# A two-layer hybrid trunk on one Trainium2 core: state-space blocks gathered by group before their products, first normed tiles placed between the row products, rotary tables and masks placed behind the last normed tile, and further hand-overs rearranged

## The chip, the cores and the metric

The kernel runs on one core of one Trainium2 chip. TensorE (PE) multiplies matrices, VectorE (DVE), ScalarE (ACT) and GpSimd (POOL) work element by element, and SyncE (SP) issues most DMA transfers; each engine follows its own list of instructions in order and waits on semaphores that the others raise. The metric is the device time of one execution in microseconds. Lower is better.

## The reference

The input x has 1024 tokens of width 1024. Two layers follow one another and a final RMSNorm ends the trunk. One layer is:

```python
mod = silu(c) @ w_ada[l] + b_ada[l]                  # six vectors of 1024: sh1, sc1, g1, sh2, sc2, g2
h = rms_norm(x, norm1_g[l]) * (1.0 + sc1) + sh1
z = h @ w_in[l]                                      # 1024 -> 512 + 256 + 128 + 32 + 1024 + 1024
u, cq_in, ckv_in, kr_in, gate_a, gate_b = split(z)
# (A) S5 mixer: 32 groups of 16 channels, 64 complex states each, a scan over the tokens
h_t = Abar * h_(t-1) + Bbar @ u_t ;  y = Re(C @ h_t) + d * u_t
y_a = (gelu(y) * sigmoid(gelu(y) @ w_glu + b_glu)) @ w_a_out
# (B) latent attention: 8 heads, 64 + 32 rotary columns, causal by positions, masked softmax
y_b = mla_mixer(cq_in, ckv_in, kr_in, positions, cos, sin, ...) @ w_b_out
merged = sigmoid(gate_a) * y_a + sigmoid(gate_b) * y_b
x = x + g1 * (merged @ w_out[l])
h = rms_norm(x, norm2_g[l]) * (1.0 + sc2) + sh2
x = x + g2 * ((silu(h @ w_gate[l]) * (h @ w_up[l])) @ w_down[l])   # inner width 2816
```

## The kernel before, in words

**Layout and precision.** Activations lie transposed, channels on the partitions: x_sb, h_hi and h_lo hold 8 tiles of 128 channels by 1024 tokens. A token half is 512 columns, half 0 and half 1. Every large product is made of three fp32r products (`products`, L550, L552, L553): weights and data are each cut into a rounded part (hi) and the remainder (lo), and hi times hi, hi times lo and lo times hi are added in PSUM. PSUM has 8 banks of 512 fp32 columns; `pair(b)` is the two banks from b on.

**Weight units.** Weights come in units of 128 x 1024 with two slots (unit number modulo 2). SP loads the raw fp32 of a unit (`load_unit`, L538, two transfers) once the remainder of unit n - 2 is made; ScalarE rounds it (`split_hi`, L526) once the raw data is there and TensorE is through with unit n - 2; GpSimd makes the remainder (`split_lo`, L534); TensorE starts the unit after `unit_ready`, which waits for the remainder. ScalarE's order inside the loops thus decides when the next unit's weights are there.

**Start.** For layer 0 VectorE makes the first two modulation vectors from rows of w_ada (`row_products`, 16 of them, SP loads the rows into the four places of ada_rows), the rotary tables after row 5 (`rope_tables`), two of the eight mask blocks after row 10 (`mask_rows`; ScalarE adds to each in `mask_block`), and two weight remainders. Then it makes normed tiles: `norm_inverse`, `hidden_scaled` and `hidden_lo` (L2032, L2042) for tile k of half o, in the order H_ORDER, with ScalarE's rounding `hidden_hi` (L1564) in between. Six mask blocks follow (L1986), and then a chain of 95 dependent small steps on [128, 32] values (`s5`, from L2077), which gives the discretised state-space parameters; ScalarE adds Exp and one Sin (L1613) to it.

**u.** TensorE makes u for half 0 while the tiles come in (`u_products`), then half 1. ScalarE evicts u in 8 steps (U_ORDER, u_t). In layer 0 ScalarE comes to them behind its mask blocks, and in both layers behind the Sin and the split of the first gate unit.

**Gate units and state-space batches.** The 16 gate units (U_GATE + t, two halves each) fill the time in which the state-space part is made. It goes by eight batches of four groups, each in four steps of half a unit (`s5_part`, part 0 to 3 at step h, b = (h - S5_LAG) / 4, with a lag of 6 half units in layer 0 and 4 in layer 1). On TensorE part 0 is `batch_transposes` (L1156: blocks be, which GpSimd makes at L933), part 1 `batch_states` (L1168, after ScalarE has copied the blocks mt, L1536, `batch_transposed`), part 3 `batch_outputs` (L1186 and L1187). The Toeplitz blocks that L1186 needs go from toe_col through DMA to toe[partition, j, r, m, g] (`batch_toeplitz`), where g, the group, is the innermost axis: the weights of one group are read 4 elements apart. L1187 reads its weights as one stretch. VectorE makes the running states with `states(b)` (L2173 and others), after TensorE's part 1, and the turned powers of the next batch.

**SP beside the gate units.** For unit t, SP issues in this order: the unit's weights, a pair of adaLN tiles (`ada_pair(t - 3)`, L642; each of the two waits until VectorE has used an earlier tile of the three in ada_raw), and for odd t `ut_load` (L703, four transfers, u by groups). VectorE uses the adaLN tiles in products that stand behind `states(b)` in its order.

**Attention.** `side_of(step)` says which query, key or value product stands between which score steps; the first pair of heads takes its values and odd keys at its steps 0 to 2.

**Merge, projection, FFN.** A merge unit multiplies attention (o_hi, o_lo) and state-space outputs (yg_hi, yg_lo) by their projection. x is spilled to HBM during a layer's first half and comes back in one transfer (x_back) ahead of the output projection, where ScalarE makes squares for the second norm. The FFN goes by chunks of two 128-row tiles: gate and up products with two bank pairs each, then `down_products`, whose eight output tiles use two bank pairs in turn, each evicted into x_sb by VectorE (L2420). Six units of weights belong to each chunk.

## Time and profile before

| | us |
|---|---|
| median of three runs | 3154.01 |
| lowest, highest | 3153.0, 3155.38 |
| profiled execution | 3150.09 |
| its span, first to last instruction | 3147.9 |
| PE busy | 3044.4 (97%) |
| PE weight load busy | 2559.9 (81%) |
| DVE busy | 1546.8 (49%) |
| ACT busy | 986.5 (31%) |
| POOL busy | 870.6 (28%) |

The mean clock granted to TensorE is 0.987 of full speed. The span of the profiled execution is 2.2 us shorter than its time: the rest lies ahead of the first instruction and behind the last. "Busy" adds up the instructions of an engine with overlaps counted once. In a row of the profile "L1168" is line 1168 of the kernel, "ps<-ut,mt" means that ps is written from ut and mt, the shapes follow in the same order, and a bracket such as [7.51 <-PE ps L1168] says that the engine stood idle for 7.51 us before the instruction and that PE's line 1168 ended the wait ("issue" is a wait that the profile puts down to nothing). All times are us from the start of the span unless ns is written.

### The profile page before, as it was taken

What the parts mean: (1) busy time and instruction counts of PE and PEld (TensorE: products, weight loads), DVE (VectorE), ACT (ScalarE), POOL (GpSimd) and SP (SyncE); (2) the same over time, 40 slices, a digit from 0 to 9 for tenths busy, and PEclk for the clock granted to TensorE, in tenths of its full rate; (3) what the DMA queues carried; (4) which work ended last, traced back from release to release, by engine and by line L of the source; (5) the groups of instructions that cost most, each with busy time, mean ns of one, the idle gap of its engine ahead of it and who ended that gap; (6) DMA issues with size and microseconds to landing.
All of it is one profiled execution on the core that took longest, in us unless ns stands there. A gap on an engine that the chain in (4) does not pass through costs nothing.

```text
span 3147.9 us, 36605 instructions
## 1 busy us (share of the span) xinstructions
PE 3044.4 (97%) x14672; PEld 2559.9 (81%) x14672; DVE 1546.8 (49%) x1949; ACT 986.5 (31%) x1397; POOL 870.6 (28%) x512
## 2 busy tenths in 40 slices
PE   6999999999999999999999999999999999999998
PEld 5787889978878888888878888898787888888886
DVE  7865487855133232232379885786524222232224
ACT  3422367751231111111142225777223111111112
POOL 0334222222422222222244542222232222222223
PEclk9999999999999999999999999999999999999999
DMA  7555400124221222111125651002331111111111
GB/s 269 170 157 156 154 13 12 51 61 155 79 75 61 62 78 63 61 61 47 47 101 168 187 175 55 14 25 51 121 135 40 51 50 47 47 47 47 48 53 67
DMA packets 278932, 264.25 MB, mean 84 GB/s; under 512 B 46706, under 2 KB 237298, under 8 KB 277619
## 3 DMA queue, kind: packets, MB, share of 16 engines
q1 hardware_dynamic: 252464, 217.66, 22.7%
q10 hardware_dynamic: 26306, 44.32, 3.8%
q8 instruction: 117, 1.92, 0.3%
q14 instruction: 45, 0.36, 0.1%
HBM read 218.59 MB, written 40.96 MB: 82 GB/s over the span
## 4 chain that ended last, share of the span: by engine, by line
PE 80%; DVE 7%; issue 5%; ACT 4%; DMA 2%; POOL 1%; SPq 1%; ACTq 1%; DVEq 0%; POOLq 0%
PE ps L550 22%; PE ps L552 22%; PE ps L553 21%; PE ps L1321 3%; PE ps L1307 2%; PE ps L1341 2%; PE ps L1342 2%; PE ps L1302 2%; PE ps L1306 2%; DVE x_sb L2420 1%; DVE silu L2402 1%; DMA raw<-in_w_in 1%; ACT hid_hi L1536 1%; PE ps L1186 1%; PE ps L1168 1%
## 5 line engine op out<-in xcount | busy, mean ns | idle before, releaser
L534 POOL TENSOR_TENSOR wlo<-raw,whi 128x1024 fp32r<-128x1024 f32 (+3 forms) x288 | 543.4, 1895 | 1963.6 <-ACT whi L526 1963.6
L526 ACT ACTIVATE whi<-raw 128x1024 fp32r<-128x1024 f32 (+3 forms) x290 | 242.8, 859 | 1637.5 <-PE ps L553 1480.5
L550 PE MATMUL ps<-h_hi,whi 128*128 128x512 f32 x2176 | 701.0, 396 | 25.8 <-DVE h_lo L2042 18.2
L552 PE MATMUL ps<-h_lo,whi 128*128 128x512 f32 x2176 | 692.3, 392 | 0.0
L553 PE MATMUL ps<-h_hi,wlo 128*128 128x512 f32 x2176 | 691.7, 392 | 0.0
L550 PEld LDWEIGHTS ps<-h_hi,whi 128*128 128x128 f32 x2176 | 409.3, 190 | 114.3 <-DVE h_lo L2042 22.2
L552 PEld LDWEIGHTS ps<-h_lo,whi 128*128 128x128 f32 x2176 | 412.8, 190 | 86.7
L553 PEld LDWEIGHTS ps<-h_hi,wlo 128*128 128x128 f32 x2176 | 411.8, 189 | 87.4
L2402 DVE TENSOR_TENSOR silu<-silu,ps 128x1024 f32<-128x1024 f32 x44 | 53.7, 1221 | 769.4 <-PE ps L553 760.2
L2420 DVE SCALAR_TENSOR_TENSOR x_sb<-ps,mod,x_sb 128x1024 f32<-128x1024 f32 x160 | 203.2, 1280 | 178.0 <-PE ps L553 178.0
L550 PE MATMUL ps<-hid_hi,whi 128*128 128x512 f32 x704 | 224.8, 393 | 9.5 <-DVE x_sb L2420 9.5
L552 PE MATMUL ps<-hid_lo,whi 128*128 128x512 f32 x704 | 222.4, 390 | 0.0
L553 PE MATMUL ps<-hid_hi,wlo 128*128 128x512 f32 x704 | 222.0, 389 | 0.0
L1916 DVE TENSOR_TENSOR pt_lo<-ps,pt_hi 128x512 fp32r<-128x512 f32 x256 | 164.5, 684 | 36.2 <-ACT pt_hi L1536 35.2
L550 PEld LDWEIGHTS ps<-hid_hi,whi 128*128 128x128 f32 x704 | 130.6, 188 | 43.8 <-DVE x_sb L2420 18.0
L1536 ACT ACTIVATE pt_hi<-ps 128x512 fp32r<-128x512 f32 x256 | 139.0, 595 | 84.8 <-PE ps L1321 83.7
L2330 DVE CUSTOM_DVE_ANT_0 ps<-ps,mask 128x1024 f32<-128x1024 f32 x128 | 157.2, 1228 | 5.2 <-PE ps L1307 2.6
L553 PEld LDWEIGHTS ps<-hid_hi,wlo 128*128 128x128 f32 x704 | 132.1, 188 | 28.1
L552 PEld LDWEIGHTS ps<-hid_lo,whi 128*128 128x128 f32 x704 | 132.2, 188 | 27.7
L1783 ACT ACTIVATE probs<-ps,neg_max 128x1024 f32<-128x1024 f32 x128 | 143.5, 1121 | 0.1
L1321 PE MATMUL ps<-ident,probs 128*128 128x128 f32 x1024 | 133.6, 273 | 2.5 <-ACT probs L1783 2.4
L1341 PE MATMUL ps<-pt_hi,v_st 128*128 128x256 f32 x512 | 128.1, 283 | 4.5 <-DVE o_un L2286 3.0
(250 smaller groups left out, 4250.9 us busy)
## 6 DMA issues: line engine op xcount, KB each, us to landing
ada_raw<-in_w_ada SPq DMA_DIRECT2D x64, 512.0 KB, 4.5
raw<-in_w_in SPq DMA_DIRECT2D x92, 256.0 KB, 4.7
raw<-in_w_gate SPq DMA_DIRECT2D x88, 256.0 KB, 3.2
raw<-in_w_up SPq DMA_DIRECT2D x88, 256.0 KB, 3.3
raw<-in_w_down SPq DMA_DIRECT2D x88, 256.0 KB, 2.8
gate_scratch<-gst ACTq DMA_DIRECT2D x32, 512.0 KB, 3.8
gl<-gate_scratch SPq DMA_DIRECT2D x32, 512.0 KB, 4.1
ada_rows<-in_w_ada SPq DMA_DIRECT2D x16, 512.0 KB, 5.6
```

What stands on the lines that cost most here:

```text
L526: last = act.activation(dst(whi[:, s, :]), src(raw[:, s, :]), ACT.Copy)
L534: last = pool.tensor_tensor(dst(wlo[:, s, :]), src(raw[:, s, :]), dst(whi[:, s, :].bitcast(F32)), ALU.subtract)
L550: pe.matmul(o, w_h, x_h, start=first, stop=False)
L552: pe.matmul(o, w_h, x_l, start=False, stop=False)
L553: return [pe.matmul(o, w_l, x_h, start=False, stop=last) for o, (x_h, _) in zip(outs, xs)]
L1321: last = pe.transpose(ps[:, 4 + t, k * P:(k + 1) * P], probs[:, T % 2, kt * P:(kt + 1) * P], ident[:, 0:P])
L1341: pe.matmul(out_, v_both, pt_hi[:, n % 2, k, :], start=(k == 0), stop=False)
L1536: return act.activation(dst, src, ACT.Copy)
L1783: act.activation(probs[:, r % 2, :], pair(2 * (r % 2)), ACT.Exp, bias=neg_max[:, r % 2:r % 2 + 1], scale=-1.0, accum_out=row_sum[:, r // T ...
L1916: return dve.tensor_tensor(out, value, hi.bitcast(F32), ALU.subtract)
L2330: dve.tensor_tensor_reduce(out=s, in0=s, in1=mask[:, step % TT, :], scale=1.0, scalar=3e38, op0=ALU.add, op1=ALU.min, accum_out=neg_max[:, ...
L2420: dve.scalar_tensor_tensor(x_sb[:, t, :], pair(2 * (t % 2)), mod[:, 5, t:t + 1], x_sb[:, t, :], ALU.mult, ALU.add).then_inc(dn_ev.sem, 1)
```

## The change

- A buffer toe_g [128, 4, 8, 16] is added. ScalarE copies the Toeplitz blocks of a batch into it, group by group (`batch_by_group`, part 2 of the batch), and raises toe_ready; TensorE's `batch_outputs` waits for toe_ready in place of toe_loaded and reads its weights as one stretch.
- In ScalarE's loop over the gate units the part at step 2t stands ahead of `split_hi` of unit t + 2 or behind it, by `turn`. The store of y (`outputs_away`) is a function of its own; for batch 7 it stands behind the latents.
- SP issues `ut_load(b)` half a lag later.
- Start: eight rows, then the modulation of tiles 0 to 3 (`first_modulation`), the first norm and the remainder of weight unit 0 (`weight_lo`, now on VectorE), then the remaining rows one by one between normed tiles; `rope_tables` and all eight `mask_rows` behind the last normed tile. TensorE puts its column sums of half 1's squares between its first products. ScalarE splits the first gate unit after mask block 5, and spills x later.
- The Sin stands among the evictions of u, behind the first two; in layer 1 the split of the first gate unit stands ahead of the second Exp.
- VectorE instead of GpSimd makes the remainders of units U_U + 1 of layer 1 and of U_FFN + 1 and U_FFN + 2 of both layers (`weight_lo`).
- The first pair's values, odd keys: one step later each.
- Merge: the yg products wait by k. Output projection: x comes back in two transfers.
- FFN: the down products use four bank pairs in turn, and the waits follow.
- End: the last column sums take the last square from the ring, without GpSimd's sum.

```diff
@@ L286
 d_col = sb("d_col", [P, G, M])
+toe_g = sb("toe_g", [P, 4, CH, M])
@@ L322
 mask_t = sb("mask_t", [P, 2, SEQ])
-place(32)
+where[0] = tables_at
 ada_rows = sb("ada_rows", [P, 4, D])
+first_c = sb("first_c", [P, D])
+place(64)
 pos_i2 = sb("pos_i2", [P, SEQ], I32)
-first_c = sb("first_c", [P, D])
...
@@ L457
 mg_ready = count("mg_ready", KT)
-x_back = count("x_back", 16)
+x_back = [count("x_back_first", 16), count("x_back_rest", 16)]
@@ L585
         if i == 0:
-            return ((VS, 0, 1), (KO, 0, 0), (KO, 0, 1), None, None, None)[g]
+            return (None, (VS, 0, 1), (KO, 0, 0), (KO, 0, 1), None, None)[g]
...
@@ L728
                 ada_pair(t - 3)
-            if t >= 3 and t % 2 and (t - 3) // 2 < 8:
-                ut_load((t - 3) // 2)
+            b, odd = divmod(t - 1 - S5_LAG[l] // 2, 2)
+            if 0 <= b < 8 and not odd:
+                ut_load(b)
@@ L1052
         add_squares(l, 1, 1, KT - 2)
-        split_lo(pool, l, U_FFN + 1)
         add_squares(l, 1, 1, KT - 1)
+        wait(pool, w_lo_done, l, U_FFN + 3)
             for j in range(6):
-                split_lo(pool, l, U_FFN + 2 + j, 3 * i)
-        for n in range(UNITS - 4, UNITS):
+                split_lo(pool, l, U_FFN + 3 + j, 3 * i)
+        for n in range(UNITS - 3, UNITS):
             add_squares(l + 1, 0, 0, k)
-        for k in range(1, KT):
+        for k in range(1, KT if l + 1 < DEPTH else KT - 1):
             add_squares(l + 1, 0, 1, k)
-        if l + 1 < DEPTH:
-            split_lo(pool, l + 1, U_U + 1)
@@ L1094
-    for half in range(2):
-        if half:
-            wait(pe, std_ready, 0, 1)
-        for k in range(KT):
+    def first_squares(half, ks):
+        for k in ks:
@@ L1110
                 last.then_inc(sq_added[half].sem, 1)
-            if half and k == 3:
-                norm_scale(0, 0)
+    first_squares(0, range(KT))
+    wait(pe, std_ready, 0, 1)
+    first_squares(1, range(2))
+    norm_scale(0, 0)
+    first_squares(1, range(2, 4))
@@ L1133
             u_products(k, [(ct, 0) for ct in U_TILES])
+            if l == 0 and k < 2:
+                first_squares(1, range(4 + 2 * k, 6 + 2 * k))
@@ L1177
             wait(pe, mat_step, l, 6 * b + 6)
-            wait(pe, toe_loaded, l, 16 * CH * (b + 1))
+            wait(pe, toe_ready, l, b + 1)
                 o = ps[:, 7, g * P:(g + 1) * P]
-                pe.matmul(o, toe[:, j, :, :, g].rearrange("p r m -> p (r m)"), ut[:, j, g, :], start=True, stop=False)
+                pe.matmul(o, toe_g[:, g, :, :].rearrange("p r m -> p (r m)"), ut[:, j, g, :], start=True, stop=False)
@@ L1403
                 tile_products(pe, j, 4 * j + 2, o_hi, o_lo, [(4 + k, k)], first=(k == 0), last=(k == PAIRS - 1))
-            if t == 0:
-                wait(pe, yg_ready, l, 4)
-            end = tile_products(pe, j, 4 * j, yg_hi, yg_lo, [(k, k) for k in range(4)])
+            for k in range(4):
+                if t == 0:
+                    wait(pe, yg_ready, l, k + 1)
+                end = tile_products(pe, j, 4 * j, yg_hi, yg_lo, [(k, k)], first=(k == 0), last=(k == 3))
@@ L1445
                             pe.wait_ge(up_done.sem, up_done.at(l, 2 * c_static - 1) + c_reg * 2)
+                            pe.wait_ge(dn_ev.sem, dn_ev.at(l, 8 * (c_static - 2) + 5 + w_i) + c_reg * 8)
+                        else:
+                            pe.wait_ge(up_done.sem, up_done.at(l, 2 * c_static) + c_reg * 2)
                             pe.wait_ge(dn_ev.sem, dn_ev.at(l, 8 * (c_static - 2) + 7 + w_i) + c_reg * 8)
-                        else:
-                            pe.wait_ge(up_done.sem, up_done.at(l, 2 * c_static) + c_reg * 2)
@@ L1459
                     t = 4 * d + nn
-                    b = 2 * (t % 2)
-                    if t < 2:
-                        pe.wait_ge(up_done.sem, up_done.at(l, 2 * c_static + (2 if last_chunk else 3)) + c_reg * 2)
-                        pe.wait_ge(dn_ev.sem, dn_ev.at(l, 8 * (c_static - 1) + 7 + t) + c_reg * 8)
+                    b = 2 * (t % 4)
+                    if t < 4:
+                        pe.wait_ge(up_done.sem, up_done.at(l, 2 * c_static + 3 + t // 2) + c_reg * 2)
                     else:
-                        pe.wait_ge(dn_ev.sem, dn_ev.at(l, 8 * c_static + t - 1) + c_reg * 8)
+                        pe.wait_ge(dn_ev.sem, dn_ev.at(l, 8 * c_static + t - 3) + c_reg * 8)
...
@@ L1527
-    mean_squares(DEPTH, 1)
+    wait(pe, sq_added[1], DEPTH, KT - 2)
+    for part in range(2):
+        if part:
+            wait(pe, sq_ready[1], DEPTH, KT)
+        for t in range(4, TT):
+            rows = (sq_sum[:, t * P:(t + 1) * P], sq_ring[:, 2 + (KT - 1) % 2, (t - 4) * P:(t - 3) * P])[part]
+            last = pe.matmul(ps[:, 6, t:t + 1], rows, mean_col[:, :], start=(part == 0 and t == 4),
+                             stop=(part == 1), skip_group_check=True)
+    last.then_inc(sq_mm.sem, 1)
@@ L1573
     norm_std(0, 0)
-    for k in range(4):
+    for k in range(2):
     split_hi(act, 0, U_U)
+    norm_rows(0, 0)
+    square(0, 0, 1, 2)
+    square(0, 0, 1, 3)
+    hidden_hi(0, 0, 0)
+    square(0, 0, 1, 4)
+    square(0, 0, 1, 5)
+    hidden_hi(0, 0, 1)
     split_hi(act, 0, U_U + 1)
-    for k in range(4, 6):
-        square(0, 0, 1, k)
-    norm_rows(0, 0)
-    for k in range(6, KT):
-        square(0, 0, 1, k)
-    for k in range(3):
-        hidden_hi(0, 0, k)
+    square(0, 0, 1, 6)
+    square(0, 0, 1, 7)
+    hidden_hi(0, 0, 2)
+    norm_std(0, 1)
@@ L1592
-        act.dma_start(xs_dram, x_sb[:, :, :]).then_inc(x_spilled.sem, 16)
+        if l:
+            act.dma_start(xs_dram, x_sb[:, :, :]).then_inc(x_spilled.sem, 16)
         hidden_hi(l, 0, 3)
-        norm_std(l, 1)
+        if l:
+            norm_std(l, 1)
             hidden_hi(l, o, k)
+            if l == 0 and (o, k) == (1, 3):
+                act.dma_start(xs_dram, x_sb[:, :, :]).then_inc(x_spilled.sem, 16)
         act.activation(sm[:, S_DT, :], ldt, ACT.Exp).then_inc(s5_act.sem, 1)
-        if l == 0:
+        if l:
+            split_hi(act, l, U_GATE)
+        else:
                 mask_block(k)
+                if k == 5:
+                    split_hi(act, l, U_GATE)
         act.activation(sm[:, S_MAG:S_MAG + 2, :], sm[:, S_AD:S_AD + 2, :], ACT.Exp).then_inc(s5_act.sem, 1)
-        wait(act, s5_dve, l, S5_ANGLES_READY)
-        act.activation(trig[:, :, :], sm[:, 0:6, :], ACT.Sin).then_inc(s5_act.sem, 1)
-        split_hi(act, l, U_GATE)
         for n, (ct, side) in enumerate(U_ORDER):
+            if n == 2:
+                wait(act, s5_dve, l, S5_ANGLES_READY)
+                act.activation(trig[:, :, :], sm[:, 0:6, :], ACT.Sin).then_inc(s5_act.sem, 1)
@@ L1635
+        def batch_by_group(b):
+            wait(act, toe_loaded, l, 16 * CH * (b + 1))
+            copy(toe_g[:, :, :, :], toe[:, b % 2, :, :, :].rearrange("p r m g -> p g r m")).then_inc(toe_ready.sem, 1)
                            ACT.Gelu_apprx_tanh).then_inc(y_gelu.sem, 1)
+            if b < 7:
+                outputs_away(b)
+        def outputs_away(b):
@@ L1654
                     batch_toeplitz(b)
+                elif part == 2:
+                    batch_by_group(b)
         for t in range(2 * KT):
-            s5_part(2 * t)
-            if t < 2 * KT:
-                split_hi(act, l, U_GATE + t + 2)
+            turn = (2 * t - S5_LAG[l]) % 4
+            if turn == 0:
+                s5_part(2 * t)
+            split_hi(act, l, U_GATE + t + 2)
+            if turn == 2:
+                s5_part(2 * t)
@@ L1703
         latent(2)
-        s5_part(4 * KT + 5)
         latent_rms(1)
+        s5_part(4 * KT + 5)
         latent_hi(2)
+        outputs_away(7)
@@ L1835
         wait(act, x_spilled, l, 16)
-        act.dma_start(x_sb[:, :, :], xs_dram).then_inc(x_back.sem, 16)
+        for part, tiles in enumerate((slice(0, 2), slice(2, KT))):
+            act.dma_start(x_sb[:, tiles, :], xs_dram[:, tiles, :]).then_inc(x_back[part].sem, 16)
             wait(act, wo_ev, l, n + 1)
+            if n == 0:
+                for part in x_back:
+                    wait(act, part, l, 16)
@@ L1995
-    for n in range(2 * KT):
+    def first_rows(n):
         row_products(mod[:, m, k:k + 1], ada_rows[:, n % 4, :], first_c[:, :]).then_inc(rows_used.sem, 1)
-        if n == 5:
-            rope_tables()
-        if n == 10:
-            dve.wait_ge(std_ready.sem, 1)
-            dve.reciprocal(rstd[:, 0, 0:4], std[:, 0, 0:4]).then_inc(rstd_ready.sem, 1)
-            for t in range(2):
-                mask_rows(t)
-        if n in (12, 14):
-            t = n // 2 - 6
-            wait(dve, w_hi_done, 0, U_U + t + 1)
-            lo_of(wlo[:, t, :], raw[:, t, :], whi[:, t, :]).then_inc(w_lo_done.sem, 1)
-    dve.wait_ge(rows_used.sem, 2 * KT)
-    for m in range(2):
-        dve.tensor_tensor(mod[:, m, :], mod[:, m, :], cols[:, 0, ROW_B_ADA + m * KT:ROW_B_ADA + (m + 1) * KT], ALU.add)\
-            .then_inc(mod_ready.sem, 1)
-    dve.wait_ge(mod_ready.sem, 2)
-    dve.scalar_tensor_tensor(a1[:, :], mod[:, 1, :], 1.0, cols[:, 0, ROW_N1:ROW_N1 + KT], ALU.add, ALU.mult)\
-        .then_inc(a1_ready.sem, 1)
+    def first_modulation(lo, hi):
+        dve.wait_ge(rows_used.sem, 2 * hi)
+        b_both = cols[:, 0, ROW_B_ADA:ROW_B_ADA + 2 * KT].rearrange("p (m k) -> p m k", m=2)
+        link(dve.tensor_tensor(mod[:, 0:2, lo:hi], mod[:, 0:2, lo:hi], b_both[:, :, lo:hi], ALU.add))
+        link(dve.scalar_tensor_tensor(a1[:, lo:hi], mod[:, 1, lo:hi], 1.0, cols[:, 0, ROW_N1 + lo:ROW_N1 + hi],
+                                      ALU.add, ALU.mult))
+        if hi == KT:
+            dve.sem_inc(mod_ready.sem, 2)
+            dve.sem_inc(a1_ready.sem, 1)
+    def weight_lo(l, n):
+        s = n % 2
+        wait(dve, w_hi_done, l, n + 1)
+        wait(dve, w_lo_done, l, n)
+        apart(dve)
+        lo_of(wlo[:, s, :], raw[:, s, :], whi[:, s, :]).then_inc(w_lo_done.sem, 1)
@@ L2042
-    wait(dve, a1_ready, 0, 0)
-    dve.wait_ge(c_stored.sem, 16)
+    for n in range(8):
+        first_rows(n)
+    first_modulation(0, 4)
+    norm_inverse(0, 0)
+    weight_lo(0, U_U)
+    first_rows(8)
+    dve.wait_ge(act_const.sem, 3)
     hidden_scaled(0, 0, 0)
-    for k in range(2):
-        hidden_lo(0, 0, k)
+    hidden_lo(0, 0, 0)
+    first_rows(9)
+    hidden_lo(0, 0, 1)
+    first_modulation(4, 5)
+    hidden_lo(0, 0, 2)
+    weight_lo(0, U_U + 1)
+    norm_inverse(0, 1)
@@ L2059
-        for k in range(2, 4):
-            hidden_lo(l, 0, k)
-        norm_inverse(l, 1)
-        for o, k in H_ORDER[4:]:
+        if l:
+            weight_lo(l, U_U + 1)
+        if l == 0:
+            for m, (o, k) in enumerate(H_ORDER[3:9]):
+                first_rows(10 + m)
+                if m == 5:
+                    first_modulation(5, KT)
+                hidden_lo(l, o, k)
+        else:
+            for k in range(2, 4):
+                hidden_lo(l, 0, k)
+            norm_inverse(l, 1)
+            for o, k in H_ORDER[4:9]:
+                hidden_lo(l, o, k)
+        for o, k in H_ORDER[9:]:
         if l == 0:
-            for k in range(2, KT):
+            dve.wait_ge(c_stored.sem, 16)
+            rope_tables()
+            for k in range(KT):
@@ L2362
-        wait(dve, x_back, l, 16)
-        apart(dve)
         for n in range(KT - 2):
+            if n in (0, 2):
+                wait(dve, x_back[n // 2], l, 16)
+                apart(dve)
@@ L2385
         last_out(KT - 1, 1)
-        for k in range(1, 6):
+        hidden_lo(l, 2, 1)
+        weight_lo(l, U_FFN + 1)
+        for k in range(2, 6):
@@ L2393
             hidden_lo(l, 3, k)
+        weight_lo(l, U_FFN + 2)
@@ L2417
                 dve.wait_ge(dn_ev.sem, dn_ev.at(l, 8 * (c_static - 1) + t + 1) + 8 * c_reg)
-                dve.scalar_tensor_tensor(x_sb[:, t, :], pair(2 * (t % 2)), mod[:, 5, t:t + 1], x_sb[:, t, :],
+                dve.scalar_tensor_tensor(x_sb[:, t, :], pair(2 * (t % 4)), mod[:, 5, t:t + 1], x_sb[:, t, :],
```

## Rows read from the trace of the kernel before

**Rows 1.** The page's first part: busy us of each engine, share, instructions

```profile
PE 3044.4 (97%) x14672; PEld 2559.9 (81%) x14672; DVE 1546.8 (49%) x1949; ACT 986.5 (31%) x1397; POOL 870.6 (28%) x512
```

**Rows 2.** Waits of PE, whole span: engine line waited for: us, times, longest us

```profile
PE ps L550 <- DVE h_lo L2042: 18.2, 10, 4.5
PE ps L1168 <- ACT mt L1536: 11.8, 4, 3.5
PE ps L550 <- DVE x_sb L2420: 9.5, 20, 0.5
PE ps L550 <- DVE yg_lo L1916: 6.9, 2, 4.0
PE ps L550 <- POOL wlo L534: 4.6, 3, 1.6
...
PE ps L1281 <- DVE v_st L1916: 3.0, 2, 1.5
```

**Rows 3.** Waits of ACT between 107 and 365

```profile
ACT whi L526 <- DMA raw<-in_w_in: 132.5, 7, 20.6
```

**Rows 4.** Timeline of SP, layer 0: start, duration, engine, line, operation

```profile
166.00 1.49 SPq L642 DMA_DIRECT2D ada_raw<-in_w_ada  x2
167.62 2.47 SPq L703 DMA_DIRECT2D ut<-u_scratch  x4
170.52 0.93 SPq L545 DMA_DIRECT2D raw<-in_w_in  x2
```

**Rows 5.** Timeline of ACT, layer 0

```profile
176.07 1.06 ACT L526 ACTIVATE whi<-raw 128x1024 fp32r<-128x1024 f32 x1 [20.62 <-DMA raw<-in_w_in]
...
183.01 0.60 ACT L1536 ACTIVATE mt<-ps 128x512 f32<-128x512 f32 x1 [2.68 <-issue]
```

**Rows 6.** Timeline of DVE, layer 0

```profile
154.31 0.69 DVE L2173 TENSOR_TENSOR z_tmp<-rot_b,ps 128x512 f32<-128x512 f32 x1 [7.51 <-PE ps L1168]
```

**Rows 7.** Timeline of PE, layer 0

```profile
153.22 1.05 PE L1168 MATMUL ps<-ut,mt 128*128 128x128 f32 x8
...
165.96 0.50 PE L1186 MATMUL ps<-ut,toe 128*128 128x128 f32 x2
```

**Rows 8.** Windows: us, busy (x) of PE PEld DVE ACT POOL, clock, DMA, GB/s

```profile
183.60:332.80 149.20, 140.97 (x660) 119.60 (x660) 90.75 (x138) 38.75 (x42) 59.39 (x40) 0.95 0.53 164
1718.00:1744.80 26.80, 26.80 (x134) 22.90 (x133) 23.45 (x28) 7.82 (x8) 13.38 (x8) 1.00 0.59 183
```

**Rows 9.** Weight loads of two lines: ns min/median/max, first and last start

```profile
L1186 PEld LDWEIGHTS ps<-ut,toe x128: 308/310/332, 165.7 to 1893.3; 128*128 128x128 f32 x128
...
L1187 PEld LDWEIGHTS ps<-h_st,m x128: 189/198/208, 166.2 to 1893.7; 128*128 128x128 f32 x128
```

**Rows 10.** Timeline of ACT, layer 1

```profile
1648.49 0.36 ACT L1613 ACTIVATE trig<-sm 128x192 f32<-128x192 f32 x1 [3.73 <-DVE sm L2086]
...
1653.64 1.22 ACT L1536 ACTIVATE u_t<-ps 128x512 f32<-128x512 f32 x2 [3.83 <-PE ps L553]
...
1704.25 1.06 ACT L526 ACTIVATE whi<-raw 128x1024 fp32r<-128x1024 f32 x1 [10.76 <-PE ps L553]
```

**Rows 11.** Timelines of POOL and PE, layer 1

```profile
1681.21 1.63 POOL L933 TENSOR_TENSOR be<-m_tmp 128x512 f32<-128x512 f32 x1
...
1685.35 0.60 PE L1156 MATMUL ps<-ident,be 128*128 128x128 f32 x4
...
1703.99 0.50 PE L1186 MATMUL ps<-ut,toe 128*128 128x128 f32 x2
```

**Rows 12.** Timelines of DVE, POOL and PE before the first states

```profile
89.24 7.50 DVE L1986 SCALAR_TENSOR_TENSOR mask_t<-pos_f,hi_bias,pos_lo 128x1024 f32<-128x1024 f32 x6 [2.78 <-ACT mask L1590]
97.95 0.19 DVE L2077 TENSOR_TENSOR sm<-s5p,sm 128x32 f32<-128x32 f32 x1 [1.22 <-ACT mask L1590]
...
138.52 1.62 POOL L933 TENSOR_TENSOR be<-m_tmp 128x512 f32<-128x512 f32 x1
...
147.31 0.60 PE L1156 MATMUL ps<-ident,be 128*128 128x128 f32 x4
```

More of the change, by code:

```diff
@@ L444, in trunk @@
         toe_loaded = count("toe_loaded", 16 * CH * 8)
+        toe_ready = count("toe_ready", 8)
         v_mm = count("v_mm", 8)
```

9 lines of the change are left out of this document (4 added, 5 removed).

## The prediction

> **What bounds the kernel now.** I read five kinds of view. The page's totals come first [rows 1]: TensorE counts as busy for 3044.4 of 3147.9 us, so no other engine is the bound, and an edit is worth the TensorE time that it removes or adds. The waits of TensorE come next [rows 2]: its idle time is a few dozen small waits, and the rows name them: first normed tiles (h_lo), the transposed blocks of the state-space part (mt), the FFN's evictions (x_sb, twenty times), the gated outputs (yg_lo), weight remainders made by GpSimd (wlo), and the attention's first values (v_st). The change aims at each of them. Then I asked who on the other engines is late, although nobody waits for it now. One row stands out: while TensorE works on layer 0's gate units, ScalarE waits seven times for a weight tile, 132.5 us in all and up to 20.6 [rows 3]. That wait costs little today. The timelines of SP, ScalarE, VectorE and TensorE around one such wait [rows 4 to 7] tell what hangs on it, and two windows [rows 8] give what one batch of four groups takes: 149.2 / 5 = 29.8 us in layer 0, 26.8 in layer 1, where TensorE is never idle. The 3.06 between them is idle time (149.2 - 140.97, over five: 1.65) and time at the lower clock (0.95 granted).
>
> **Blocks copied by group, layer 0.** `batch_outputs` of TensorE now waits for `toe_ready`, a copy that ScalarE makes in `batch_by_group`. In ScalarE's order this copy stands behind `split_hi` of unit t + 2. In layer 0 (lag 6) batch 0's copy thus stands behind the split of gate unit 6. That split is the one that waits for its transfer [rows 5]: it starts at 176.07, while TensorE starts the outputs at 165.96 [rows 7]. Why is the transfer late? SP issues it only behind two adaLN transfers, and these wait for products that VectorE makes after `states(0)` [rows 4, 6]: states from 154.31, adaLN transfers issued at 166.00 and until 167.49, then four ut transfers, then the weights at 170.52, landed when the split starts 5.55 later. The change takes only the ut transfers out of the way. The new order: 167.5 + 5.55, and 0.4 for the adaLN data now right ahead: 173.5; the split 1.06 [rows 5]; the copy, of 512 elements as the mt copy, 0.60 [rows 5]; 0.1 for the hand-over: 175.3. TensorE waits from 165.96: 9.3 us. The whole chain starts with TensorE's own products for states (153.22) and comes back to them, so it cannot be worked off earlier: it repeats for batches 0 to 5. Batch 6 escapes, as its copy stands ahead of the next split.
>
> What a batch loses and gains. The blocks are contiguous: a strided weight load takes 310 ns where its neighbour takes 198 [rows 9], with eight loads a batch, 8 x 0.112 = 0.9 us saved. The mt waits (1.65 a batch) and their slow clock (1.4) go, 3.06 in all. A 9.3 us pause brings a slow clock of its own; between today's 1.4 and twice that and more, since the pause is thrice as long: I take 2.4, bounds 1.4 and 3.4. Sum: 9.3 - 0.9 - 3.06 + 2.4 = 7.7 us a batch, six times: **+46** (bounds 38 and 56, with 0.5 either way for the landing). The step from batch 6 to 7 loses its 3.06 and gains 0.9, less 1 for the clock still low: -3; batch 7 saves 0.9, and the later gelu some 0.6 at the latent norms: **-4.5** together.
>
> A page bears on the saving. The strided load of the trace costs 310 against 198 ns for the same 128 columns [rows 9]. The Trainium skill ("TensorE: Matmul & The Clock Gate", LDWEIGHTS) makes the load a matter of the column count alone, so the copy would save nothing; "SBUF — State Buffer" (Door 1, on cachelines) says that fp32 read 16 bytes apart pays at every element, which is this stride. The measured rows side with the second page.
>
> **The same copy in layer 1** (lag 4). No transfer is late here, but the split itself cannot start before TensorE ends unit t: it starts at 1704.25 [rows 10], with TensorE's outputs due at 1703.99 [rows 11]. 1704.25 + 1.06 + 0.60 + 0.1 = 1706.0, a wait of 2.0. Less 0.9: 1.1 a batch for seven batches, and 0.8 each for the clock (bounds 0 and 1.7); batch 7 saves 0.9: 7.7 + 5.6 - 0.9 = **+12** (7 to 19).
>
> **Sine behind two evictions.** In layer 1 the Sin now stands behind the copies of u's first two banks, which begin with TensorE's last k step: 1653.64 + 1.22 [rows 10], a DMA issue of about 0.3, then the table load that moves along, then 0.36. VectorE's chain of 95 steps waits for it. It comes at 1655.6 without the table load and near 1656.9 with it, instead of 1648.85: 6.7 to 8.0 late. The blocks be are ready at 1682.84 and TensorE asks at 1685.35 [rows 11]: slack 2.5. A stall of 4.2 to 5.5 and a slow clock of 1.4 to 2.8: **+7.5** (5.6 to 8.3).
>
> **Start.** First tiles between the row products let TensorE begin its products some 10 us earlier. But six rope operations and eight mask rows, of at most 1.25 us each ([rows 12]: 7.50 for six), now all stand behind the last normed tile. There is no less VectorE work, only another order. Before, VectorE was through with the tiles at 89.24 - 2.78 = 86.46, and the state-space chain began at 97.95 (both [rows 12]). By the same durations I get the last tile at 84 (VectorE now waits for rows, for squares and for the first scale), then 7 + 10 us, and 3 to 4 for GpSimd's remainders in between and ScalarE's split among the masks: the chain begins near 104. ScalarE too reaches u's evictions only behind the masks, near 106, so the gate units start about where they do now. The chain was ready 7.2 us ahead of TensorE (138.52 + 1.62 against 147.31, [rows 12]) and pays with that slack. One of GpSimd's remainders falls outside the chain (-2). So **0** at the first transposes (bounds -5, if the last tile comes at 79, and +4, if it comes at 88).
>
> **Small terms**, each with what comes next. Outputs by k in the merge: both yg_lo waits (6.9, [rows 2]) and two slow-clock stretches (2 x 1.4) go; unit 1's remainder is due next, 0.9: **-8.8** (-6 to -10.5). FFN down products over four bank pairs: the third product takes the banks of the second up tile, free since VectorE's multiply, so the twenty x_sb waits go: 9.5 by the row, which counts from modelled ends: **-11** (-9.5 to -12.8). Remainders on VectorE instead of GpSimd: the three wlo waits, 4.6, go but 0.7, and 1.1 twice of the h_lo waits, as GpSimd no longer holds VectorE up: **-6** (-2 to -9). Values one step later: the v_st waits of 3.0 and what follows: **-4** (0 to -6). Last square straight from the ring: **-0.7**. x_back in two parts, the moved spill and output transfers: no TensorE wait stands there today, so 0, with +1 if ScalarE is held before its squares.
>
> **Sum**: 46 - 4.5 + 12 + 7.5 + 0 - 8.8 - 11 - 6 - 4 - 0.7 = +30.5 us. Against the profiled execution (3150.09, of which 3147.9 is the span) that is 3180.6; its median of runs is 3.9 higher, 3154.01, so I forecast 3154.0 + 30.5 = **3184.5 us**.
>
> **Rivals.**
> 1. *The transfer is in time* (the other side). With the ut transfers behind the weights, SP might reach the weights before VectorE's states. Then layer 0 behaves as layer 1: 2.0 - 0.9 - 3.06 + 0.8 = -1.2 a batch, -7 instead of +46: 3131. It decides at the landing: once the tile lands before 165.96 the stall is 2.0; each later us costs six. For it: the ut transfers took 2.9 of the 4.5 us between the adaLN issue and the weights. Against it: SP stood still until 166.00, when the first of the two products was ready, and the change leaves these waits where they are. 9%.
> 2. *The clock costs more.* Half speed for twice as long after each long pause, and in layer 1 after every 2 us wait: 6 x 1 + 7 x 0.9 = +12: 3197. For it: today's pauses of 2.5 to 3.5 us already lower the clock in layer 0. Against: several did not. 12%.
> 3. *The early start is kept.* The chain begins at 97 after all and nothing later takes it back: -7: 3177. Against: the sum of VectorE's work. 8%.
> 4. *Contiguous blocks save nothing*: 16 x 0.9 = 14.4 more: 3199. This is what the column count alone would give; the rows speak against it. 2%.
>
> **Chances and range.** My forecast 69%, with its own range 3170 to 3199 (terms: 9 for layer 0's batches, 5 each for the start, layer 1 and the small ones). Runs of this kernel lie within 0.1%, and 0.2%, 6.3 us, is what can be told from no change. Slower than 3160.3 hold the forecast and rivals 2 to 4 but for their tails: 0.87. Faster is rival 1 and a little of a shorter stall: 0.10. Between: 0.03. The range that leaves about two in ten out, mostly rival 1 and the top of rival 2: 3160 to 3203.
>
> **What would show it.** The waits of TensorE should have a new row, outputs (line of the toe_g product) waiting for ScalarE's copy: some 9 us six times and 2 us seven times, about 70 us in all; the page's PE share falls to 95 or 96%. ScalarE's waits for raw stay above 100 us in layer 0. The distance between TensorE's states products should be near 37.5 us in layer 0 and 28 to 29 in layer 1. Strided loads of 310 ns should be gone. x_sb, yg_lo and mt should have left the waits. Layer 1's transposes should wait some 5 us for be. The state-space chain should begin near 104, the gate units near 107. I am wrong in the main step if the first of the long waits is under 4 us, and wrong in the start if the first transposes move by over 5 us.

## The result, and the profile after

The changed kernel takes 3191.6 us (median, 3186.8 to 3193.7), the kernel before 3154.7 in the same series: ratio 1.0114, 95% interval 1.0096 to 1.0131. A second series gave 3194.7 against 3150.6, ratio 1.0136 (1.0120 to 1.0151). It is slower by 1.0 to 1.5%. The forecast was 3184.5 (3160 to 3203), a rise of 30.5 us where 36.9 and 44.2 were measured. The two traced executions lie 42.8 us apart in span (3147.9 and 3190.7); the places below add up to that figure.

The totals of the page, kernel after, answer to [rows 1]. TensorE is busy for 9 us less and the span is 42.8 longer, so the added time is idle time of TensorE; what its lower clock costs lies inside the busy time:

```profile
span 3190.7 us, 36615 instructions
...
PE 3035.3 (95%) x14680; PEld 2555.4 (80%) x14680; DVE 1549.3 (49%) x1957; ACT 1000.7 (31%) x1412; POOL 863.3 (27%) x506
```

The waits of TensorE over the whole span, kernel after (us in all, times, longest), against [rows 2]:

```profile
PE ps L1191 <- issue: 71.1, 13, 9.8
...
PE ps L553 <- DVE h_lo L2086: 13.0, 9, 2.7
PE ps L1173 <- DMA ut<-u_scratch: 6.8, 1, 6.8
PE ps L553 <- ACT u_t L1549: 6.0, 1, 6.0
PE ps L1326 <- ACT probs L1822: 5.9, 4, 2.2
...
PE ps L1161 <- POOL be L936: 3.0, 1, 3.0
PE ps L1173 <- ACT mt L1549: 2.8, 1, 2.8
PE ps L553 <- POOL wlo L537: 2.5, 2, 1.9
```

L1191 is the product with toe_g. The row says "issue", not ScalarE, so the releaser has to be read from the start and end times: ScalarE's timeline in layer 0 shows the copy ending at 180.87 + 1.10 = 181.97, TensorE's shows the product starting at 182.07.

```profile
179.90 1.06 ACT L529 ACTIVATE whi<-raw 128x1024 fp32r<-128x1024 f32 x1 [17.67 <-DMA raw<-in_w_in]
180.87 1.10 ACT L1549 ACTIVATE toe_g<-toe 128x512 f32<-128x512 f32 x1
```

```profile
182.07 0.77 PE L1191 MATMUL ps<-ut,toe_g 128*128 128x128 f32 x2 [7.46 <-issue]
...
219.29 0.77 PE L1191 MATMUL ps<-ut,toe_g 128*128 128x128 f32 x2 [9.49 <-issue]
```

The copy stands behind a split that waits 17.67 us for its weights, while its own blocks had landed by 169.5. SP's timeline around the first copy shows why the weights are late, in the same order as [rows 4] but for the ut transfers: weights issued at 174.28, only after two adaLN transfers that VectorE let go at 172.74. (ada_raw has two places, not three.)

```profile
172.74 1.49 SPq L645 DMA_DIRECT2D ada_raw<-in_w_ada  x2
174.28 0.97 SPq L548 DMA_DIRECT2D raw<-in_w_in  x2
```

The windows of the kernel after (columns as in [rows 8]): four batches of layer 0 and one of layer 1. A layer 0 batch takes 150.25 / 4 = 37.6 us, where [rows 8] give 29.8; the clock is 0.86 against 0.95. TensorE falls to 1.2 GHz for 10.2 us around each of the five long waits from the second on (212.69 to 222.93 around the one that ends at 219.29) and for 6.8 us around the first, where before it fell for 6.8 us around three of the four waits for mt.

```profile
219.25:369.50 150.25, 111.89 (x528) 94.87 (x529) 74.44 (x110) 35.30 (x37) 47.88 (x33) 0.86 0.43 131
1747.20:1777.20 30.00, 27.73 (x132) 23.17 (x132) 23.27 (x28) 8.84 (x10) 13.38 (x9) 0.94 0.53 163
```

Start times of the same TensorE work in the two traces give the balance. "Shift" is the lateness of the changed kernel at that point.

| point | before | after | shift |
|---|---|---|---|
| first u product | 56.65 | 44.80 | -11.9 |
| first transposes of layer 0 | 147.31 | 145.93 | -1.4 |
| states(0), layer 0 | 153.22 | 158.79 | +5.6 |
| states(6), layer 0 | 332.88 | 384.48 | +51.6 |
| first scores | 411.39 | 463.84 | +52.5 |
| merge, first product | 682.78 | 735.40 | +52.6 |
| first down product | 964.22 | 1009.69 | +45.5 |
| first transposes of layer 1 | 1685.35 | 1724.54 | +39.2 |
| states(0), layer 1 | 1691.26 | 1732.10 | +40.8 |
| states(7), layer 1 | 1878.55 | 1937.33 | +58.8 |
| first down product, layer 1 | 2489.70 | 2541.07 | +51.4 |

### The profile page after: what moved, and what is told of

Same layout as the page of the kernel before. It is cut to its first block, busy times and chain, and to the rows that moved or that the text cites. A ratio compares the mean times of both kernels' runs of the same rounds, so it can differ in the third digit from the quotient of the medians.

```text
span 3190.7 us, 36615 instructions
## 1 busy us (share of the span) xinstructions
PE 3035.3 (95%) x14680; PEld 2555.4 (80%) x14680; DVE 1549.3 (49%) x1957; ACT 1000.7 (31%) x1412; POOL 863.3 (27%) x506
## 4 chain that ended last, share of the span: by engine, by line
PE 86%; DVE 6%; issue 3%; ACT 2%; DMA 1%; POOL 1%; SPq 0%; ACTq 0%; DVEq 0%; POOLq 0%
PE ps L553 23%; PE ps L555 23%; PE ps L556 23%; PE ps L1326 3%; PE ps L1346 2%; PE ps L1347 2%; PE ps L1312 2%; PE ps L1307 2%; PE ps L1311 2%; DVE t_ring L2076 1%; PE ps L1102 1%; DVE h_lo L2086 1%; PE ps L1191 1%; PE ps L1192 1%; PE ps L1173 0%
## 5 line engine op out<-in xcount | busy, mean ns | idle before, releaser
L537 POOL TENSOR_TENSOR wlo<-raw,whi 128x1024 fp32r<-128x1024 f32 (+3 forms) x283 | 533.7, 1894 | 1993.3 <-ACT whi L529 1993.3
```

The lines of the kernel that those rows point to most:

```text
L537: last = pool.tensor_tensor(dst(wlo[:, s, :]), src(raw[:, s, :]), dst(whi[:, s, :].bitcast(F32)), ALU.subtract)
```

## The experiments

Theory A was that the copy costs only by its place behind a split whose weights are late.

**The copy ahead of the split** (changed kernel):

```diff
-                    turn = (2 * t - S5_LAG[l]) % 4
-                    if turn == 0:
-                        s5_part(2 * t)
+                    s5_part(2 * t)
                     split_hi(act, l, U_GATE + t + 2)
-                    if turn == 2:
-                        s5_part(2 * t)
```

> The changed kernel with one thing undone: in ScalarE's loop over the gate units every part at step 2t stands ahead of the split of unit t + 2, the copy by group too. Theory A (the copy costs because of what it stands behind): the 13 waits of TensorE's outputs (71.1 us) go, layer 0's states come 28.9 us apart instead of 37.4 and layer 1's 25.9 instead of 28.4 to 30; 6 x 8.5 + 7 x 3.4 = 75 less than 3191.6: 3117 us (3108 to 3126). Rival B (the copy costs wherever it stands, because its own blocks land late): ScalarE waits for toe ahead of the split, the waits of the outputs stay above 40 us in all, and the time above 3165 us.

Measured: 3126.5 us (3124.4 to 3129.3), ratio to before 0.9924 (0.9907 to 0.9941), above the 3117 that was expected. The order of two calls is worth some 62 to 69 us (36.9 or 44.2 over the kernel before against 24.8 under it; the spans lie 68.1 apart). The windows, one batch of layer 0 and one of layer 1: layer 1 at 25.90, as expected; layer 0 at 30.35, where 28.9 was expected: there the miss lies.

```profile
219.20:249.55 30.35, 29.33 (x132) 24.56 (x132) 19.59 (x27) 8.96 (x9) 12.00 (x8) 0.89 0.52 159
1740.00:1765.90 25.90, 25.90 (x134) 22.01 (x133) 23.30 (x27) 8.95 (x9) 13.41 (x8) 1.00 0.63 189
```

Rival B falls, though one of its signs is there: ScalarE does wait for the blocks, 50.4 us in layer 0. TensorE's outputs wait only 3.1 us for it, and the kernel with both edits below has the same wait (53.1) with batches of 25.9 us, so it does not set the time.

```profile
ACT toe_g L1549 <- DMA toe<-toe_col: 50.4, 7, 7.9
```

What is left in layer 0 are waits at the states product, as before the change. The last of these rows is the wait of the outputs for the copy:

```profile
PE ps L1173 <- issue: 9.2, 3, 4.4
PE ps L1173 <- ACT mt L1549: 7.0, 4, 2.7
PE ps L1173 <- DMA ut<-u_scratch: 6.5, 1, 6.5
PE ps L1191 <- ACT toe_g L1549: 3.1, 3, 1.4
```

**Layer 0's adaLN pairs one gate unit later** (changed kernel, copy still behind the split):

```diff
-                    if 3 <= t < 2 * KT + 3:
-                        ada_pair(t - 3)
+                    first = 3 if l else 4
+                    if first <= t < 2 * KT + first:
+                        ada_pair(t - first)
```

> The changed kernel, the copy still behind the split, with SP issuing layer 0's pairs of adaLN tiles one gate unit later, so that a weight unit no longer stands behind a pair that waits for VectorE. Theory A (the weights are late only by SP's order): ScalarE's wait for raw falls from 131 us to under 40, the outputs' waits in layer 0 fall from 9.6 to 2.4 us as in layer 1, and ut for batch 0 comes a place earlier, so that its 6.8 us wait goes: 6 x 8.4 + 6 = 56 less, 3135 us (3125 to 3145). Rival C (the transfers are late because the DMA engines are loaded): the wait stays above 90 us and the time above 3175 us.

Measured: 3130.4 us (3127.0 to 3130.9), ratio 0.9931 (0.9914 to 0.9947). The first row is TensorE's wait, the second ScalarE's between 100 and 450 (130.9 in the changed kernel between 100 and 420). In this listing L1192 is the line of the product with toe_g.

```profile
PE ps L1192 <- issue: 27.2, 12, 2.3
```

```profile
ACT whi L529 <- DMA raw<-in_w_in: 8.1, 1, 8.1
```

The DMA engines were not too busy (rival C); the weights were late by SP's order alone.

**No copy, blocks read 4 elements apart** (changed kernel):

```diff
-                    wait(pe, toe_ready, l, b + 1)
+                    wait(pe, toe_loaded, l, 16 * CH * (b + 1))
-                        pe.matmul(o, toe_g[:, g, :, :].rearrange("p r m -> p (r m)"), ...)
+                        pe.matmul(o, toe[:, j, :, :, g].rearrange("p r m -> p (r m)"), ...)
-                        elif part == 2:
-                            batch_by_group(b)
```

> The changed kernel without the copy: TensorE reads the Toeplitz blocks as before, 4 elements apart, and waits for their transfer; all else stays. Theory A: the outputs' waits go as in the kernel with the copy ahead, and the strided loads of 310 ns come back, 0.9 us a batch: 14.4 us more than that kernel, about 3131 us. Rival D (a load costs by its columns alone, so contiguous blocks save nothing): equal to that kernel within 3 us.

Measured: 3133.3 us (3129.8 to 3135.6), ratio 0.9940 (0.9924 to 0.9957): 6.9 above the kernel with the copy ahead (its own ratio 0.9924), about half of the 14.4 that A gave. The weight loads of the product, here and with the copy ahead:

```profile
L1191 PEld LDWEIGHTS ps<-ut,toe x128: 308/310/332, 175.4 to 1892.4; 128*128 128x128 f32 x128
```

```profile
L1191 PEld LDWEIGHTS ps<-ut,toe_g x128: 186/192/192, 174.2 to 1883.5; 128*128 128x128 f32 x128
```

In layer 1, states products lie 26.75 us apart here and 25.88 with the copy: 0.87 a batch, the predicted 0.9. In layer 0, where the batch is set by the late weights, states(0) to states(7) take 214.4 us here and 215.3 there: the faster loads save nothing. Rival D falls; A forgot that a saving on an engine that waits anyway is only a longer wait.

**The copy behind the split, alone, in the kernel before:**

```diff
+        toe_g = sb("toe_g", [P, 4, CH, M])
+        toe_ready = count("toe_ready", 8)
...
+                elif part == 2:
+                    batch_by_group(b)
...
+                    turn = (2 * t - S5_LAG[l]) % 4      # as in the change
```

> The kernel before with the copy by group alone, placed behind the split of unit t + 2 in both layers, nothing else changed. Theory A: TensorE waits some 9 to 10 us for it in six batches of layer 0 and 2.4 us in seven of layer 1; 46 - 4.5 + 15 over 3154.7: 3211 us (3200 to 3222). Rival E (the slow batches need the later ut transfers or another part of the change as well): under 3185 us.

Measured: 3231.5 us (3229.2 to 3232.9), ratio 1.0252 (1.0235 to 1.0269). No other part is needed for the slow batches (rival E falls), but it costs 80 us over the kernel before of its series (3151.2), 24 more than A had and outside its range. The wait is longer than in the changed kernel, and SP's timeline shows by what: four ut transfers stand between the adaLN pair and the weights.

```profile
256.72 0.77 PE L1188 MATMUL ps<-ut,toe_g 128*128 128x128 f32 x2 [11.64 <-issue]
```

```profile
244.98 1.49 SPq L644 DMA_DIRECT2D ada_raw<-in_w_ada  x2
246.66 2.48 SPq L705 DMA_DIRECT2D ut<-u_scratch  x4
249.17 1.00 SPq L547 DMA_DIRECT2D raw<-in_w_in  x2
```

So the later ut transfers, another part of the change, pay in each slow batch. The next run undoes them alone.

**The ut transfers at their old places** (changed kernel):

```diff
-                    b, odd = divmod(t - 1 - S5_LAG[l] // 2, 2)
-                    if 0 <= b < 8 and not odd:
-                        ut_load(b)
+                    if t >= 3 and t % 2 and (t - 3) // 2 < 8:
+                        ut_load((t - 3) // 2)
```

> The changed kernel with SP's ut transfers back at the places they had before (layer 0: one gate unit earlier, between a batch's adaLN pair and the next weights; layer 1 unchanged). Theory F (the later ut transfers pay in each slow batch and cost once): the wait for ut at the first states (6.8 us and some lower clock) goes, but the weights of six batches land behind four more transfers, so that the outputs' waits rise from 9.6 to 12 us as in the run with the copy alone: 6 x 2.6 - 7 = +8.6, 3200 us (3194 to 3206). Rival G (the place of the ut transfers matters only for the first batch): 3185 us (3181 to 3188).

Measured: 3201.1 us (3197.7 to 3201.8), ratio 1.0156 (1.0142 to 1.0170). Between 107 and 450 TensorE now waits 68.3 / 6 = 11.4 us for each copy, a batch takes 39.7 us on average (37.6 in the changed kernel), and the wait for ut is gone. By the two spans it ends 5.5 us later than the changed kernel; by the medians it is 6.4 above the second series of it and 9.5 above the first, from different series.

```profile
PE ps L1190 <- issue: 68.3, 6, 11.5
PE ps L1172 <- ACT mt L1548: 4.4, 1, 4.4
```

Rival G falls.

**The Sin back ahead of u's evictions** (changed kernel):

```diff
+                wait(act, s5_dve, l, S5_ANGLES_READY)
+                act.activation(trig[:, :, :], sm[:, 0:6, :], ACT.Sin).then_inc(s5_act.sem, 1)
                 wait(act, x_spilled, l, 16)
                 for n, (ct, side) in enumerate(U_ORDER):
-                    if n == 2:
-                        ...
```

> The changed kernel with the Sin back ahead of u's first evictions in both layers. Theory H: layer 1's transposes no longer wait for be (3.0 us) nor run at the lower clock behind it: 3 to 5 us less, 3187 us, all of it at the first transposes of layer 1. Rival I (the wait comes from the new place of layer 1's first gate split or of the weight remainder on VectorE, not from the Sin): within 1 us of 3191.6.

Measured: 3186.6 us (3184.6 to 3189.3), ratio 1.0114 (1.0099 to 1.0130), which beside the two series of the changed kernel (1.0114, 1.0136) settles nothing. The traces do. TensorE reaches layer 1's transposes without a wait; in the changed kernel it waits for be at half clock:

```profile
1719.46 0.60 PE L1161 MATMUL ps<-ident,be 128*128 128x128 f32 x4
```

```profile
1724.54 0.92 PE L1161 MATMUL ps<-ident,be 128*128 128x128 f32 x4 [2.97 <-POOL be L936]
```

Rival I falls for this wait. Its price in time comes from a later pair of runs. In layer 0, where this run moves the Sin back too, ScalarE comes later to u's evictions and TensorE's wait for u_t grows from 6.0 to 11.4 us. TensorE then no longer waits for ut, and its states product starts at 157.03, against 158.79: there the longer wait takes the place of another.

```profile
PE ps L553 <- ACT u_t L1549: 11.4, 1, 11.4
```

**Four bank pairs for the down products, alone, in the kernel before:**

```diff
-                            b = 2 * (t % 2)
-                            if t < 2:
+                            b = 2 * (t % 4)
+                            if t < 4:
...                         # and the waits that go with it, as in the change
```

> The kernel before with the FFN's down products over four bank pairs and the waits that go with it, nothing else. Theory J: the twenty waits for x_sb go, 0.64 us by the distance of the matmuls each: 3151.2 - 12 = 3139 to 3143 us, some 6 us per layer. Rival K (as many waits appear at the gate and up products, which reuse the banks): within 2 us of 3151.

Measured: 3136.9 us (3133.5 to 3137.8), ratio 0.9950 (0.9937 to 0.9964): 14.7 less. Windows over the first to the last down product of layer 0, kernel before and this one:

```profile
964.20:1605.60 641.40, 636.49 (x2801) 523.18 (x2799) 202.72 (x165) 108.66 (x112) 153.14 (x69) 1.00 0.19 59
```

```profile
968.90:1602.40 633.50, 633.31 (x2801) 524.14 (x2799) 202.67 (x165) 108.60 (x112) 153.07 (x69) 1.00 0.19 59
```

7.9 us a layer, of which only 4.7 is idle time; the other 3.2 is counted as busy. No wait appears at the gate and up products (rival K falls), and the gain is above the 8 to 12 that J gave.

**Both edits, copy ahead and adaLN pairs later:**

> The changed kernel with both the copy by group ahead of the split and layer 0's adaLN pairs one gate unit later. Theory A: in layer 0 neither the copy nor the blocks mt wait behind a late transfer, so layer 0's batches take 25.9 us as layer 1's (30.8 with the copy ahead alone), 7 x 4.9 = 34 less, and the 6.5 us wait for ut goes: 3126.5 - 40 = 3086 us (3080 to 3095). Rival L (another chain, VectorE's rotations and scans, sets 28.7 us a batch as in the run with the later pairs alone): 3106 us.

Measured: 3083.0 us (3082.0 to 3083.7), ratio 0.9782 (0.9767 to 0.9797). Six batches of layer 0, states(1) to states(7), leave TensorE no idle time at full clock: 25.9 us each.

```profile
178.00:333.30 155.30, 155.30 (x793) 131.68 (x792) 140.33 (x165) 54.77 (x55) 80.50 (x48) 1.00 0.60 182
```

Rival L falls: VectorE is busy for 140 of 155 us, close to a bound but not yet one.

**The changed kernel again, and two further edits, on one chip:**

> The changed kernel once more, on one chip with the two below, for comparison: 36 to 38 us over the kernel before, 3188 us beside a kernel before of 3151.

Measured: 3194.7 us (3190.6 to 3196.3), 44 over the kernel before of that series, where 36 to 38 were expected.

```diff
-                    if n == 2:                          # Sin in the loop over u's evictions
+                    if n == (0 if l else 2):
```

> The copy ahead of the split, layer 0's adaLN pairs one gate unit later, and the Sin ahead of u's evictions in layer 1 alone. Theory H: layer 1's transposes no longer wait 3.0 us for be and no lower clock follows: 3 to 5 us under the kernel with the first two edits alone (3083.0): 3079 us (3076 to 3082). Rival: layer 1's wait moves to the next product that needs the state-space chain, no gain: 3083 us.

Measured: 3078.6 us (3078.1 to 3079.9), ratio 0.9772 (0.9758 to 0.9785): 4.4 under the kernel with two edits by the medians; by their traces the states of layer 1 move from 1647.39 to 1642.88, 4.5. The rival falls.

```diff
+        place(128)                                      # first_c no longer where tq is written
         first_c = sb("first_c", [P, D])
...
             first_modulation(4, 5)
+            rope_tables()
             hidden_lo(0, 0, 2)
...
-                    rope_tables()                       # behind the last normed tile
```

> The kernel b2_sin_by_layer with the rotary tables made ahead of the third normed tile, where VectorE of the changed kernel waits 4.6 us for ScalarE and 1.7 for the next scale; first_c lies in other memory for that. Theory M (the early first tiles are worth nothing at the gate units because VectorE's tables and masks follow them in one piece of 18 us): 5 to 7 us of it move into the idle time, the state-space chain begins near 97 instead of 103, TensorE's wait for u_t (6.0 us) nearly goes, the third tile comes 3 us later at TensorE: 4 to 6 us less, 3074 us (3072 to 3077). Rival N (the gate units and transposes are held by something else, or the later third tile costs as much): within 1 us of b2_sin_by_layer.

Measured: 3071.6 us (3070.1 to 3075.2), ratio 0.9751 (0.9738 to 0.9765), 7.0 under the kernel without it, where 4 to 6 were expected. The gap used is VectorE's 4.62 in the changed kernel (first fence); with the tables in it, the third tile comes only 1.3 us later and the chain begins at 97.29 instead of 103.32 (second fence). TensorE's wait for u_t goes.

```profile
52.67 0.75 DVE L2086 SCALAR_TENSOR_TENSOR h_lo<-t_ring,mod,h_hi 128x512 fp32r<-128x512 f32 x1 [4.62 <-ACT h_hi L1577]
...
103.32 0.51 DVE L2145 TENSOR_TENSOR sm<-s5p,sm 128x32 f32<-128x32 f32 x1 [1.74 <-ACT mask L1607]
```

```profile
53.98 0.75 DVE L2084 SCALAR_TENSOR_TENSOR h_lo<-t_ring,mod,h_hi 128x512 fp32r<-128x512 f32 x1
...
97.29 0.57 DVE L2143 TENSOR_TENSOR sm<-s5p,sm 128x32 f32<-128x32 f32 x1 [1.75 <-ACT mask L1609]
```

Rival N falls.

**The first pair's values at their old steps** (the version before this one, with `side_of` as before the change):

> The kernel b3_rope_in_gap with the first pair's values and odd keys back at their old steps. Theory O (the later step saves nothing, its wait only changes its name): the waits for v_st (1.5 us a layer) and a first one for probs (0.5) come back and the new one for probs (2.2 us a layer) goes, so within 1.5 us of b3_rope_in_gap: 3071 us (3070 to 3073). Rival, the step as the prediction costed it: 2 us a layer more, 3075.6 us.

Measured: 3073.5 us (3072.1 to 3076.1), ratio 0.9753 (0.9740 to 0.9767) against 0.9751. The values wait again for v_st, and the longest wait for probs falls from 2.2 to 0.8:

```profile
PE ps L1328 <- ACT probs L1820: 3.4, 5, 0.8
...
PE ps L1288 <- DVE v_st L1957: 2.9, 2, 1.5
```

The medians lie 1.9 apart, in different series; each measured against its own kernel before, the difference is 0.8. By the traces the stretch from the first scores to the glu products takes 0.4 us (layer 0) and 0.3 us (layer 1) less with the old steps. One wait has only changed its name; the rival, 2 us a layer for the later step, falls.

## Why the prediction was right, point by point

The sign and the place were right, and the main step came out by its own working. Each term beside what the two traces show:

| step | predicted | measured | by |
|---|---|---|---|
| layer 0, batches 0 to 6 | +46 | +46.0 | states(0) to states(6) |
| layer 0, batch 6 to the scores | -4.5 | +0.8 | states(6) to first scores |
| layer 1, batches | +12 | +15.6 | states(0) to first scores |
| Sine in layer 1 | +7.5 | +4.5 | run with the Sin by layer |
| start | 0 | +5.6 | states(0); transposes -1.4 |
| merge by k | -8.8 | -9.1 | glu products to output projection, both layers |
| FFN banks | -11 | -15.8 | down products, first to last, both layers |
| remainders | -6 | about -6 | three stretches between the others |
| values | -4 | 0 (+1.7 in the traces) | run with the old steps |
| end | -0.7 | -0.6 | last down product to the end |

With +1.7 for the values the measured terms add up to 42.7 of the 42.8 us. They do so by construction: the remainders are what is left of three stretches once the other terms are taken out, so that row alone is no measurement of its own. The total is in part offset: the start, the end of layer 0's batches, layer 1 and the values cost 20.2 us more than forecast, while the banks and the Sin took 7.8 back.

**Layer 0's copy.** A wait of 9.3 us was forecast, six times; measured were 7.5 at the first, which TensorE reaches later because it runs at 1.2 GHz until 164.9 behind the wait for ut, and 9.5 to 9.8 at the other five. A batch of 37.5 us was forecast, and 38.1 for the first and 37.4 to 37.7 for the others measured. The chain was read in the right order: TensorE's states, VectorE, SP's queue, the split, the copy. Rival 1 (the transfer in time) did not come about: SP still reached the weights only after VectorE. The clock term was 2.4, between 1.4 and 3.4; with no wait and full clock a batch takes 25.9, so the 37.4 hold 9.65 of wait (by the distance of the matmuls) and 1.9 of clock. That the six batches came to 46.0 where 46 was forecast is in part luck: the wait was 0.35 too short, the clock 0.5 too dear, and the first batch 0.6 longer than the others. Rival 2 fell with it in layer 0; in layer 1 the clock took 1.6 us four times, 0.9 a batch where 0.8 was put.

**What failed: the start, put at 0 because its sum ended at the first transposes.** There it held (-1.4), and so did its parts (last tile at 83.3 where 84 was forecast, chain at 103.3 where 104 was). But the prediction looked no further than the transposes. The change issues the ut transfers of batch 0 behind one more adaLN pair, at 153.24, and states(0) waits for them:

```profile
158.79 1.62 PE L1173 MATMUL ps<-ut,mt 128*128 128x128 f32 x6 [6.78 <-DMA ut<-u_scratch]
```

The prediction had counted the move of these transfers only as a gain for the weights behind them (weights issued 3 us earlier, 2.6 after the adaLN data in front; the run with the old places shows 11.4 against 9.5 us of wait, 2.1 a batch) and never asked who waits for what was moved. With the transfers at their old places the states start at 151.01. Rival 3 (the early start kept) fell: the chain began at 103.3.

**What the late weights cost before.** "That wait costs little today" was too kind to them. In the kernel before the blocks mt are copied behind the same late split [rows 5], so its layer 0 batches take 3.2 us more than those of layer 1 (29.94 against 26.76 by the distance of the states products, the waits for mt being the only ones in them). The prediction priced those waits (3.06 a batch) without tying them to the transfer. With both edits, in the changed kernel, they are gone.

**Sizes that were off.** The copy takes 1.10 us, not the 0.60 of a copy with the same number of elements [rows 5]: so 2.26 us of wait in layer 1, not 2.0 (2.42 by the distance of the matmuls), and the clock fell behind four of the seven waits, which makes batches of 30.0 us of those and 28.4 of the others. That is most of what layer 1 cost beyond the forecast. Between batch 6 and the scores the wait for mt did not go (2.79 us at 413.33) and the latent squares ran at half clock behind it. Each of the ten FFN waits a layer cost 0.64 by the distance of the matmuls, and the first product behind it another 0.11, where the step went by the idle row and by the distances; together 7.5 of the 7.9 a layer; the rest was not traced further. The Sin ended 6.5 us later than in the run with the Sin at its old place, relative to u (forecast 6.7 to 8.0), but the blocks be only 5.6, so that the wait was 3.0 and not 4.2 to 5.5: 5.6 less the slack, which was 2.5 as forecast. The values' step priced the wait removed and not the one behind it, the probabilities, which then came 2.2 us late.

**Contiguous blocks.** 310 against 192 ns a load, 0.87 us a batch where TensorE is the bound and nothing where it waits. Rival 4 fell. "TensorE: Matmul & The Clock Gate" of the Trainium skill (LDWEIGHTS), by which the columns alone set the load, does not describe these loads; "SBUF — State Buffer" (Door 1) of the Trainium skill, by which each access that crosses to a new 16-byte line pays, agrees with these rows in the sign.

**The best version run** holds the change with the copy ahead of the split, layer 0's adaLN pairs one unit later, the Sin late in layer 0 alone, and the rotary tables in VectorE's gap: 3071.6 us, 2.5% under the kernel before. The change without the copy's place behind the split was worth 24.8 us; that place hid it. How much of the rest belongs to the change is not shown: no run puts the later adaLN pairs into the kernel before, whose own layer 0 batches waited behind the same late weights.

## What to carry to other kernels

Before a small operation is put into an in-order queue, read what the instruction ahead of it waits for, not what it costs: here 1.1 us of copy became 7.5 us of wait once and 9.5 us or more five times, through a transfer whose lateness had cost some 3 us a batch until then. When a transfer is moved for the sake of what stands behind it, look up the first instruction that reads what was moved. And a saving counts only in the stretches where its engine does not wait: the same faster loads gave 0.87 us a batch in layer 1 and nothing in layer 0.

## What the runs showed of the hardware beyond what was expected

A copy on ScalarE that reads fp32 of SBUF 16 bytes apart and writes it densely, 128 x 512, took 1.10 us; a dense one of the same size, which reads PSUM (mt), took 0.60. No run separates the stride from the source.

A wait of about 2.3 us lowered TensorE's clock to 1.2 GHz for 3.4 us in four of seven cases at the same place in the code; the five waits of 9.5 to 9.8 us did so for 10.2 us each time. The slow stretch did not simply grow with the wait: it was 6.8 us around the wait of 7.5, and 10.2 around the one of 6.8 for ut and around the one of 2.8 for mt in layer 0.

Where a wait was short and often repeated (0.48 us idle, ten times a layer), its removal gave 7.9 us where the idle time was 4.7: here the row of the wait was a lower bound of its price.
